# Latent attention: transposed blocks in two PSUM banks, narrow scores in one shared bank

## The chip, the cores and the metric

The program runs on one core of one Trainium2 chip. The metric is the device time of that core in microseconds (us). Three runs of the kernel before took 3803.45, 3799.05 and 3801.53 us; the median is 3801.53 us.

## The reference, cut to what matters

The program is two transformer blocks in one launch. The first has differential attention, a mixture of experts and a pooling mixer. The second runs its layer twice, and each layer has retention, latent attention and gated linear attention side by side. The change lies in the routine that computes both kinds of attention, and moves work in the latent one, which runs twice (once for each layer):

```python
def block(args):                       # one block of 128 queries
    qn, qp, i0 = args
    sc = (jnp.einsum('bqhd,bkhd->bhqk', qn, k_nope)
          + jnp.einsum('bqhd,bkd->bhqk', qp, k_pe)).astype(jnp.float32) * scale
    q_chunk = (i0 + jnp.arange(Q_BLOCK)) // CHUNK
    mask = key_chunk[None, :] <= q_chunk[:, None]
    sc = jnp.where(mask, sc, -jnp.inf)
    p = jax.nn.softmax(sc, axis=-1).astype(v.dtype)
    return jnp.einsum('bhqk,bkhe->bqhe', p, v)
```

There are 8 heads, 1024 positions, 96 columns (64 and 32) in queries and keys, and 64 in values. A block of queries sees the keys of its own chunk of 64 and of those before it.

## The kernel before, in words

`phase_attention` (L610) serves both kinds: `maps == 2` (the flag `diff`) is the differential one, `maps == 1` the latent one, whose tiles are named `mla_...` in the profile. What follows is the latent case.

**Tiling.** A head has 8 tiles of 128 queries. They are taken in pairs, a wide one (tile 7 - i, which sees 8 - i blocks of 128 keys) and a narrow one (tile i, which sees i + 1 blocks), for i = 0 to 3. A step n is one such pair; a head has 4 steps, a phase has 32, and i = n % 4. Every step therefore handles 9 blocks.

**What a step does.** TensorE computes the scores of the pair (`scores`, L734) and adds the mask by a last small product (L751). VectorE takes the negated row maxima, wide first and then narrow (`maxima`, L895, instructions L901 and L909). ScalarE computes the exponentials and their row sums (`exp`, L830, instruction L833). TensorE transposes the blocks of probabilities (L722), ScalarE copies them from PSUM to `aT` (`copy_t`, L826, instruction L828), and TensorE multiplies them by the values (`outputs`, L765, instruction L769). VectorE divides by the row sums (`scaled_out`, L927, instruction L935), which empties `o_ps`. In each step TensorE also transposes half of the keys or of the queries of a later head, the turn (`turn`, L725): at i = 0 the second half of the next head's keys, at i = 1 and 2 its queries, at i = 3 the first half of the keys of the head after it. ScalarE copies turned keys (L823), VectorE turned queries (L884). The last heads have no turn: a phase has 7 turns each at i = 0, 1 and 2, and 6 at i = 3.

**PSUM.** Of the eight banks the scores take six, three for each parity of n: two wide and one narrow. One bank, `tp`, takes all transposed blocks. One, `o_ps`, takes the outputs.

**Order.** Each engine's order is written out by hand. TensorE's (L784 to L811), with its waits:

1. the scores of step n + 1, wide and then narrow (each part waits for the exponentials of the same part two steps earlier; the first step of a head also waits for the copies of its keys and queries, L736);
2. the first four wide blocks of step n are transposed;
3. the narrow outputs of step n - 1, behind a wait for the narrow copy (L774);
4. wait for the copy of the first four; the remaining 4 - i wide blocks are transposed into the same bank;
5. wait for `o_done` (L801), that is for `scaled_out(n - 1)`; then the wide outputs of the first four blocks;
6. wait for the copy of the remaining wide blocks; the turn, into the same bank;
7. the wide outputs of the remaining blocks;
8. wait for the copy of the turn (L810); the i + 1 narrow blocks are transposed.

ScalarE's order in step n is: copy of the first four, exponentials of wide n + 1, copy of the remaining wide blocks, copy of turned keys, copy of the narrow blocks, exponentials of narrow n + 1. VectorE's is: reciprocals (L925), maxima of n + 1 (wide, narrow), `scaled_out(n - 1)`, copy of turned queries. The waits are for counted semaphores. Products of 32-bit tiles show as two records each in the trace, transposes as one.

Of the kernel before, what the change touches and what calls it, by code (L numbers as in the profile page):

```python
# [15 lines left out]
P = 128  # L16
# [6 lines left out]
HEADS = 8  # L23
# [586 lines left out]
def phase_attention(nc, K, name, q, k, v, out, maps, dk, dv, mask, scale, totals, early, lam_parts=None, prefetch=None, out_rows=None):  # L610
# [12 lines left out]
    B0, B1, SM = 0, 4, 8  # L623

# [10 lines left out]
    with Phase(nc, name) as ph:  # L635
# [8 lines left out]
        s_ps = ph.ps("s", [P, 6 * HALF])  # L644
        tp = ph.ps("tp", [P, 4, P])
# [13 lines left out]
        def scores_of(n, part, mp):  # L659

            at = (mp * 2 + (4 - mp) * part if diff else n % 2 * 3 + 2 * part) * HALF
            return s_ps[:, at:at + (tiles_of(n)[part] + 1) * P]
# [9 lines left out]
        with nc.Block() as block:  # L672
# [46 lines left out]
            def _(pe):  # L719
                def transposes(pieces, ready):  # L720
                    for n, piece in enumerate(pieces):
                        last = nc.tensor.transpose(tp[0:piece.shape[-1], n, :], piece, K["ident"])  # L722
                    last.then_inc(ready, 1)

                def turn(what, part, h):  # L725

                    if what == "k":
                        pe.wait_ge(k_in, 16 * h + 16)
                        transposes([ks[:, 4 * part + t, :] for t in range(4)], k_ready)
                    else:  # L730
                        pe.wait_ge(q_in, 16 * h + 16)
                        transposes([qs[:, 4 * part + t, :] for t in range(4)], q_ready)

                def scores(n):  # L734
                    h = n // PAIRS
                    if n % PAIRS == 0:  # L736
# [40 lines left out]
                spare = tp[:, :, :].rearrange("p a b -> p (a b)")  # L777
# [4 lines left out]
                scores(0)  # L782
# [33 lines left out]
            def _(act):  # L816
# [4 lines left out]
                def copy_k(part, h):  # L821
                    act.wait_ge(k_ready, 2 * h + part + 1)
                    act.copy(kT[h % 2][:, part * HALF:(part + 1) * HALF].rearrange("p (n c) -> p n c", n=4),  # L823
                             tp[0:dq, :, :]).then_inc(k_copied, 1)

                def copy_t(n, g, at, count):  # L826
                    act.wait_ge(t_ready, 3 * n + g + 1)
                    act.copy(aT[:, at:at + count, :], tp[:, 0:count, :]).then_inc(t_copied, 1)  # L828
# [20 lines left out]
                copy_k(0, 1)  # L849
# [3 lines left out]
                for n in range(N):  # L853
                    i = n % PAIRS
                    ahead = n + 1 < N
                    copy_t(n, 0, B0, 4)
# [4 lines left out]
                    copy_t(n, 1, B1, 4 - i)  # L861
# [3 lines left out]
                    if what == "k" and h < HEADS:  # L865
                        copy_k(part, h)
                    copy_t(n, 2, SM, i + 1)
# [10 lines left out]
            def _(dve):  # L878
                ch = Chain(dve, own)

                def copy_q(part, h):
# [3 lines left out]
                                      tp[0:dq, :, :], scale, None, ALU.mult).then_inc(q_copied, 1)  # L885
# [2627 lines left out]
```

## Time and profile before

| | |
|---|---|
| median of three runs (lowest, highest) | 3801.53 us (3799.05, 3803.45) |
| span of the profiled execution | 3803.4 us |
| own time of the profiled execution | not listed apart from the span |
| TensorE busy, of the span | 3550.1 us, 93% |
| TensorE weight loads, of the span | 2743.8 us, 72% |
| VectorE / ScalarE / GpSimd busy | 61% / 49% / 9% |
| mean granted TensorE clock | 0.976 |
| the latent-attention phases | about 2677 to 2887 us and 3391 to 3602 us |
| the differential phase | about 294 to 536 us |

The span runs from the first to the last instruction of one profiled execution. It is 1.9 us above the median of the runs and inside their spread, so differences worked out in the trace are taken from the median without a correction. "PEld" is TensorE's loading of the stationary operand, which runs ahead of the products; its rows give the moment at which TensorE reaches a group of instructions. A line of the timeline holds a group of like instructions: its start, the time it covers, the engine, the line, the tile, the shapes and the count. The bracket at its end is idle time of the engine ahead of it, and what ended that.

### The profile page before, as it was taken

Reading aid. Unit: us, or ns where it says so; the run is one execution under the profiler, and the core shown is the slowest. Engines: PE = TensorE matmul, PEld = TensorE weight load, DVE = VectorE, ACT = ScalarE, POOL = GpSimd, SP = SyncE. Lnnn points to the kernel's source line nnn. Section 1 sums busy time; section 2 is a strip of 40 time slices with the busy share of each in tenths; the row PEclk is TensorE's granted clock in tenths of the full one; section 3 lists DMA queues with packets and bytes.
Section 4 is the critical chain, followed back from the end, with each engine's and each line's share of the span. In section 5 each row is a group of like instructions: output and inputs, shape, how many; then the busy total and the mean of one; then the engine's idle time right before and its main releaser. Section 6 shows DMA issues by size and latency. Waiting matters only on the chain. (4 is left out here: it accounts for less than half of the span.)

```text
span 3803.4 us, 53075 instructions
## 1 busy us (share of the span) xinstructions
PE 3550.1 (93%) x18079; PEld 2743.8 (72%) x18079; DVE 2327.9 (61%) x3676; ACT 1876.9 (49%) x3147; POOL 334.8 (9%) x379
## 2 busy tenths in 40 slices
PE   8998889899999989999999998999998989999888
PEld 7885658688777735677887775778775767887666
DVE  3227866699888666548988885750235745313375
ACT  3115652388788610116888884321446623224574
POOL 0000002000000020001000002200002200000032
PEclk9999999899999999999999999999999999999999
DMA  6323224499999885428999997442322344232132
GB/s 241 105 69 101 68 84 167 150 398 398 399 398 399 307 319 206 152 105 300 398 399 398 398 399 288 151 175 68 109 48 80 108 139 171 106 107 63 50 114 81
DMA packets 408607, 781.27 MB, mean 205 GB/s; under 512 B 99296, under 2 KB 154232, under 8 KB 406392
## 3 DMA queue, kind: packets, MB, share of 16 engines
q1 hardware_dynamic: 385400, 695.15, 50.6%
q0 software_dynamic: 13824, 50.34, 3.5%
q10 hardware_dynamic: 9216, 33.56, 2.2%
q8 instruction: 104, 1.70, 0.2%
q14 instruction: 63, 0.52, 0.0%
HBM read 643.00 MB, written 135.95 MB: 205 GB/s over the span
## 5 line engine op out<-in xcount | busy, mean ns | idle before, releaser
L247 DVE TENSOR_TENSOR experts_gate_lo<-weights_gate,experts_gate_hi 128x1024 fp32r<-128x1024 f32 x256 | 300.7, 1221 | 75.3 <-ACT experts_gate_hi L243 62.0
L247 DVE TENSOR_TENSOR experts_down_lo<-weights_down,experts_down_hi 128x1024 fp32r<-128x1024 f32 x256 | 302.2, 1222 | 46.2 <-ACT experts_down_hi L243 42.9
L243 ACT CAST experts_gate_hi<-weights_gate 128x1024 fp32r<-128x1024 f32 x256 | 258.2, 1055 | 125.1 <-DMA weights_gate<-in_moe_w_gate_dram 70.4
L247 DVE TENSOR_TENSOR experts_up_lo<-weights_up,experts_up_hi 128x1024 fp32r<-128x1024 f32 x256 | 297.5, 1219 | 3.3 <-ACT experts_up_hi L243 2.6
L312 PE MATMUL project_acc<-project_wh,project_hh 128*128 128x512 f32 (+2 forms) x768 | 286.3, 373 | 0.0
L314 PE MATMUL project_acc<-project_wh,project_hl 128*128 128x512 f32 (+2 forms) x768 | 282.1, 367 | 0.0
L313 PE MATMUL project_acc<-project_wl,project_hh 128*128 128x512 f32 (+2 forms) x768 | 282.0, 367 | 0.0
L243 ACT CAST experts_up_hi<-weights_up 128x1024 fp32r<-128x1024 f32 x256 | 259.1, 1056 | 43.6 <-DMA weights_up<-in_moe_w_up_dram 41.1
L243 ACT CAST experts_down_hi<-weights_down 128x1024 fp32r<-128x1024 f32 x256 | 260.1, 1052 | 33.9 <-DMA weights_down<-in_moe_w_down_dram 33.2
L2582 ACT COPY project_row<-project_acc 128x512 f32<-128x512 f32 (+2 forms) x96 | 51.9, 541 | 364.3 <-PE project_acc L314 364.3
L312 PE MATMUL experts_gp<-experts_gate_hi,experts_xh 128*128 128x512 f32 x512 | 202.8, 396 | 25.2 <-DVE experts_xl L247 25.1
L312 PE MATMUL experts_yp<-experts_down_hi,experts_hTh 128*128 128x512 f32 x512 | 204.6, 400 | 2.8 <-DVE experts_hTl L247 2.8
L312 PE MATMUL experts_up<-experts_up_hi,experts_xh 128*128 128x512 f32 x512 | 204.9, 400 | 0.0
L901 DVE TENSOR_REDUCE mla_bias<-mla_s 128x1 f32<-128x1024 f32 (+1 forms) x64 | 65.6, 1025 | 225.7 <-PE mla_s L751 225.7
L314 PE MATMUL experts_up<-experts_up_hi,experts_xl 128*128 128x512 f32 x512 | 200.2, 391 | 0.0
L313 PE MATMUL experts_up<-experts_up_lo,experts_xh 128*128 128x512 f32 x512 | 199.8, 390 | 0.0
L314 PE MATMUL experts_gp<-experts_gate_hi,experts_xl 128*128 128x512 f32 x512 | 199.8, 390 | 0.0
L313 PE MATMUL experts_yp<-experts_down_lo,experts_hTh 128*128 128x512 f32 x512 | 199.6, 390 | 0.0
L313 PE MATMUL experts_gp<-experts_gate_lo,experts_xh 128*128 128x512 f32 x512 | 199.5, 390 | 0.0
L314 PE MATMUL experts_yp<-experts_down_hi,experts_hTl 128*128 128x512 f32 x512 | 199.4, 389 | 0.0
L828 ACT COPY mla_aT<-mla_tp 128x384 f32<-128x384 f32 (+1 forms) x192 | 92.0, 479 | 189.7 <-PE mla_tp L722 189.5
L312 PEld LDWEIGHTS project_acc<-project_wh,project_hh 128*128 128x128 f32 x768 | 145.2, 189 | 20.4 <-issue 0.5
(520 smaller groups left out, 8254.7 us busy)
## 6 DMA issues: line engine op xcount, KB each, us to landing
weights_gate<-in_moe_w_gate_dram SPq DMA_DIRECT2D x256, 512.0 KB, 13.4
weights_up<-in_moe_w_up_dram SPq DMA_DIRECT2D x256, 512.0 KB
weights_down<-in_moe_w_down_dram SPq DMA_DIRECT2D x256, 512.0 KB, 13.5
scratch_y<-experts_y ACTq DMA_DIRECT2D x64, 512.0 KB
pool_shared<-in_ada_w_dram SPq DMA_DIRECT2D x16, 1536.0 KB
scratch_proj<-project_row SPq DMA_DIRECT2D x64, 256.0 KB, 2.0
head_store<-in_attn_w_qkv_dram SPq DMA_DIRECT2D x48, 256.0 KB, 3.3
scratch_qkv<-qkv_row SPq DMA_DIRECT2D x48, 256.0 KB, 2.0
```

Of the source, the lines that this page charges most:

```text
L243: return act.copy(hi, src)
L247: return dve.tensor_tensor(lo, src, hi.bitcast(F32), ALU.subtract)
L312: nc.tensor.matmul(acc, a[0][k], b[0][k], start=(start and k == 0), stop=False)
L313: nc.tensor.matmul(acc, a[0][k], b[1][k], start=False, stop=False)
L314: last = nc.tensor.matmul(acc, a[1][k], b[0][k], start=False, stop=(stop and k == n - 1))
L828: act.copy(aT[:, at:at + count, :], tp[:, 0:count, :]).then_inc(t_copied, 1)
L901: dve.tensor_reduce(bias[:, n % 2, mp:mp + 1], scores_of(n, 0, mp), AX.X, ALU.max, negate=True).then_inc(bias_ready, 1)
L2582: act.copy(row[:, n % SLOTS, 0:width(s)], acc[:, n % AB, 0:width(s)]).then_inc(acc_done, 1)
```

## The change

For `maps == 1` alone, `tp` becomes two banks, FRONT and BACK. The first four wide blocks and the turn go to FRONT, the remaining wide blocks and the narrow blocks to BACK. Each group of transposes waits for the copy of the group that used its bank last (`bank_free`). The bank comes from the scores: wide scores keep two banks for each parity, narrow scores of all steps share one, so narrow scores of n + 1 wait for the exponentials of narrow n, and not of n - 1. They are issued behind the transposes of the first four wide blocks of n. The wait for the copy of the first four moves from the remaining transposes to the wide outputs, the wait for the copy of the remaining blocks from ahead of the turn to behind it. For `maps == 2` the number of banks, the order and the conditions stay, and two waits in a step are repeated. The body of TensorE's loop and the helpers (the calls of ScalarE and VectorE change only by the bank they name):

```diff
+    BANKS = 1 if diff else 2
+    FRONT, BACK = BANKS - 1, 0
-        s_ps = ph.ps("s", [P, 6 * HALF])
-        tp = ph.ps("tp", [P, 4, P])
+        s_ps = ph.ps("s", [P, (6 if diff else 5) * HALF])
+        tp = ph.ps("tp", [P, BANKS, 4, P])
...
-            at = (mp * 2 + (4 - mp) * part if diff else n % 2 * 3 + 2 * part) * HALF
+            if diff:
+                at = (mp * 2 + (4 - mp) * part) * HALF
+            else:
+                at = (4 if part else n % 2 * 2) * HALF
...
+                def copied(n, use):
+
+                    if n < 0:
+                        return (k_copied, 3) if use == 3 else None
+                    what, part, ahead = turned(n)
+                    if use != 2:
+                        return t_copied, 3 * n + min(use, 2) + 1
+                    if ahead < HEADS:
+                        return k_copied if what == "k" else q_copied, 2 * ahead + part + 1
+                    return copied(n, use - BANKS)
+
+                def bank_free(n, use):
+                    what = copied(n, use - BANKS) if use >= BANKS else copied(n - 1, use + 4 - BANKS)
+                    if what is not None:
+                        pe.wait_ge(*what)
...
-                def scores(n):
+                def scores(n, parts):
...
-                    before = n - 1 if diff else n - 2
-                    for part, i in enumerate(tiles_of(n)):
+                    for part in parts:
+                        i = tiles_of(n)[part]
+                        before = n - 1 if diff or part else n - 2
...
                     if n + 1 < N:
-                        scores(n + 1)
+                        scores(n + 1, (0, 1) if diff else (0,))
                     a_wait(n, 0)
-                    if n > 0:
-                        pe.wait_ge(t_copied, 3 * n)
-                    else:
-                        pe.wait_ge(k_copied, 3)
-                    transposes(blocks(n, 0, range(4)), t_ready)
+                    bank_free(n, 0)
+                    transposes(FRONT, blocks(n, 0, range(4)), t_ready)
+                    if n + 1 < N and not diff:
+                        scores(n + 1, (1,))
                     if n > 0:
                         narrow_outputs(n - 1)
-                    pe.wait_ge(t_copied, 3 * n + 1)
-                    transposes(blocks(n, 0, range(4, TILES - i)), t_ready)
+                    bank_free(n, 1)
+                    transposes(BACK, blocks(n, 0, range(4, TILES - i)), t_ready)
                     if i == 0:
                         pe.wait_ge(v_in[h % 2], 16 * (h // 2) + 16)
                     if n > 0:
                         pe.wait_ge(o_done, n)
+                    pe.wait_ge(t_copied, 3 * n + 1)
                     outputs(n, 0, range(4), B0)
-                    pe.wait_ge(t_copied, 3 * n + 2)
                     what, part, ahead = turned(n)
                     if ahead < HEADS:
+                        bank_free(n, 2)
                         turn(what, part, ahead)
+                    pe.wait_ge(t_copied, 3 * n + 2)
                     outputs(n, 0, range(4, TILES - i), B0)
                     a_wait(n, 1)
-                    if ahead < HEADS:
-                        pe.wait_ge(k_copied if what == "k" else q_copied, 2 * ahead + part + 1)
-                    transposes(blocks(n, 1, range(i + 1)), t_ready)
+                    bank_free(n, 3)
+                    transposes(BACK, blocks(n, 1, range(i + 1)), t_ready)
```

## Rows read from the trace of the kernel before

**Rows 1.** The page: the span.

```profile
span 3803.4 us, 53075 instructions
```

**Rows 2.** Busy time by stretch: the two latent phases; TensorE, loads, VectorE, ScalarE, GpSimd, clock, DMA.

```profile
2676.80:2887.00 210.20, 191.27 (x1235) 151.70 (x1236) 67.61 (x142) 101.09 (x244) 0.00 (x0) 0.98 0.26 70
3391.00:3602.00 211.00, 190.41 (x1241) 150.39 (x1240) 67.53 (x142) 100.47 (x244) 0.00 (x0) 1.00 0.26 70
```

**Rows 3.** Groups by line, first latent phase: loads for wide, then narrow transposes; idle last.

```profile
L722 PEld LDWEIGHTS mla_tp<-constants,mla_wide 128*128 128x128 f32 x208 | 22.3, 142 | 15.1 <-ACT mla_aT L828 11.0 <-issue 2.8
...
L722 PEld LDWEIGHTS mla_tp<-constants,mla_narrow 128*128 128x128 f32 x80 | 8.8, 144 | 11.0 <-issue 10.8
```

**Rows 4.** Timeline of TensorE's loads, the step n with i = 2 (n + 1 has i = 3).

```profile
2749.63 0.43 PEld L722 LDWEIGHTS mla_tp<-constants,mla_wide 128*128 128x128 f32 x4 [0.24 <-issue]
2750.02 0.53 PEld L769 LDWEIGHTS mla_o_ps<-mla_v,mla_aT 128*128 128x128 f32 x4
2750.97 0.20 PEld L722 LDWEIGHTS mla_tp<-constants,mla_wide 128*128 128x128 f32 x2 [0.42 <-ACT mla_aT L828]
2751.14 0.97 PEld L769 LDWEIGHTS mla_o_ps<-mla_v,mla_aT 128*128 128x128 f32 x8
...
2752.41 0.53 PEld L769 LDWEIGHTS mla_o_ps<-mla_v,mla_aT 128*128 128x128 f32 x4
2753.53 0.31 PEld L722 LDWEIGHTS mla_tp<-constants,mla_narrow 128*128 128x128 f32 x3 [0.59 <-issue]
2753.80 0.30 PEld L748 LDWEIGHTS mla_s<-mla_kT,mla_qT 96*128 96x128 f32 x2
```

**Rows 5.** The same timeline, from the three steps that follow (i = 3, 0, 1).

```profile
2757.72 0.97 PEld L769 LDWEIGHTS mla_o_ps<-mla_v,mla_aT 128*128 128x128 f32 x8 [0.26 <-DVE mla_o L935]
...
2758.99 0.30 PEld L769 LDWEIGHTS mla_o_ps<-mla_v,mla_aT 128*128 128x128 f32 x2
2759.99 0.42 PEld L722 LDWEIGHTS mla_tp<-constants,mla_narrow 128*128 128x128 f32 x4 [0.70 <-issue]
...
2764.56 0.97 PEld L769 LDWEIGHTS mla_o_ps<-mla_v,mla_aT 128*128 128x128 f32 x8 [0.26 <-issue]
...
2770.68 0.97 PEld L769 LDWEIGHTS mla_o_ps<-mla_v,mla_aT 128*128 128x128 f32 x8
2771.66 0.39 PEld L722 LDWEIGHTS mla_tp<-constants,mla_q 128*96 128x96 f32 x4
2772.03 0.75 PEld L769 LDWEIGHTS mla_o_ps<-mla_v,mla_aT 128*128 128x128 f32 x6
2773.14 0.20 PEld L722 LDWEIGHTS mla_tp<-constants,mla_narrow 128*128 128x128 f32 x2 [0.36 <-issue]
```

**Rows 6.** Timeline of VectorE, the same four steps.

```profile
2749.89 0.69 DVE L909 TENSOR_REDUCE mla_bias<-mla_s 128x1 f32<-128x512 f32 x1 [0.15 <-PE mla_s L751]
2750.79 0.29 DVE L935 TENSOR_TENSOR mla_o<-mla_o_ps,mla_ratio 128x128 f32<-128x128 f32 x1 [0.21 <-PE mla_o_ps L769]
2752.72 0.69 DVE L884 TENSOR_SCALAR mla_qT<-mla_tp 96x512 f32<-96x512 f32 x1 [1.64 <-PE mla_tp L722]
...
2757.37 0.29 DVE L935 TENSOR_TENSOR mla_o<-mla_o_ps,mla_ratio 128x128 f32<-128x128 f32 x1
...
2764.16 0.29 DVE L935 TENSOR_TENSOR mla_o<-mla_o_ps,mla_ratio 128x128 f32<-128x128 f32 x1 [0.48 <-PE mla_o_ps L769]
...
2769.44 0.55 DVE L909 TENSOR_REDUCE mla_bias<-mla_s 128x1 f32<-128x384 f32 x1
2770.03 0.29 DVE L935 TENSOR_TENSOR mla_o<-mla_o_ps,mla_ratio 128x128 f32<-128x128 f32 x1
```

**Rows 7.** Timeline of ScalarE: end of the longest narrow exponentials, and the copy after the first scores.

```profile
2755.07 0.20 ACT L833 ACTIVATION_READ_ACCUMULATOR mla_narrow<-mla_s,mla_bias 128x1 f32 x1
...
2685.80 0.59 ACT L828 COPY mla_aT<-mla_tp 128x512 f32<-128x512 f32 x1 [3.29 <-PE mla_tp L722]
```

**Rows 8.** Timeline of TensorE's loads: the first wide outputs of the phase.

```profile
2686.83 0.97 PEld L769 LDWEIGHTS mla_o_ps<-mla_v,mla_aT 128*128 128x128 f32 x8
```

More of the change, by code:

```diff
@@ L719, in _, with transposes @@
             def _(pe):
-                def transposes(pieces, ready):
+                def transposes(bank, pieces, ready):
                     for n, piece in enumerate(pieces):
-                        last = nc.tensor.transpose(tp[0:piece.shape[-1], n, :], piece, K["ident"])
+                        last = nc.tensor.transpose(tp[0:piece.shape[-1], bank, n, :], piece, K["ident"])
                     last.then_inc(ready, 1)
+                def copied(n, use):
[11 more added lines that the diff above has]
+                        pe.wait_ge(*what)
                 def turn(what, part, h):
@@ L728, in turn @@
                         pe.wait_ge(k_in, 16 * h + 16)
-                        transposes([ks[:, 4 * part + t, :] for t in range(4)], k_ready)
+                        transposes(FRONT if h > 1 or part else BACK, [ks[:, 4 * part + t, :] for t in range(4)], k_ready)
                     else:
                         pe.wait_ge(q_in, 16 * h + 16)
-                        transposes([qs[:, 4 * part + t, :] for t in range(4)], q_ready)
-                def scores(n):
+                        transposes(FRONT, [qs[:, 4 * part + t, :] for t in range(4)], q_ready)
+                def scores(n, parts):
                     h = n // PAIRS
-                    if n % PAIRS == 0:
+                    if n % PAIRS == 0 and 0 in parts:
                         pe.wait_ge(k_copied, 2 * h + 2)
                         pe.wait_ge(q_copied, 2 * h + 2)
-                    before = n - 1 if diff else n - 2
-                    for part, i in enumerate(tiles_of(n)):
+                    for part in parts:
+                        i = tiles_of(n)[part]
+                        before = n - 1 if diff or part else n - 2
                         if before >= 0:
@@ L775, in narrow_outputs @@
                     outputs(n, 1, range(n % PAIRS + 1), SM).then_inc(o_ready, 1)
-                spare = tp[:, :, :].rearrange("p a b -> p (a b)")
+                spare = tp[:, FRONT, :, :].rearrange("p a b -> p (a b)")
                 pe.sem_inc(k_ready, 2)
@@ L781, in _ @@
                     pe.wait_ge(masks_ready, 2)
-                scores(0)
+                scores(0, (0, 1))
                 turn("k", 0, 1)
@@ L819, in _, with copy_k, copy_t @@
                     act.copy(maskr[:, :], mask).then_inc(masks_ready, 1)
-                def copy_k(part, h):
+                def copy_k(bank, part, h):
                     act.wait_ge(k_ready, 2 * h + part + 1)
                     act.copy(kT[h % 2][:, part * HALF:(part + 1) * HALF].rearrange("p (n c) -> p n c", n=4),
-                             tp[0:dq, :, :]).then_inc(k_copied, 1)
-                def copy_t(n, g, at, count):
+                             tp[0:dq, bank, :, :]).then_inc(k_copied, 1)
+                def copy_t(n, g, bank, at, count):
                     act.wait_ge(t_ready, 3 * n + g + 1)
-                    act.copy(aT[:, at:at + count, :], tp[:, 0:count, :]).then_inc(t_copied, 1)
+                    act.copy(aT[:, at:at + count, :], tp[:, bank, 0:count, :]).then_inc(t_copied, 1)
                 def exp(n, part, mp):
@@ L848, in _ @@
                         exp(0, part, mp)
-                copy_k(0, 1)
+                copy_k(BACK, 0, 1)
                 if diff:
@@ L855, in _ @@
                     ahead = n + 1 < N
-                    copy_t(n, 0, B0, 4)
+                    copy_t(n, 0, FRONT, B0, 4)
                     if diff and n > 0:
@@ L860, in _ @@
                         exp(n + 1, 0, 0)
-                    copy_t(n, 1, B1, 4 - i)
+                    copy_t(n, 1, BACK, B1, 4 - i)
                     if ahead and diff:
@@ L865, in _ @@
                     if what == "k" and h < HEADS:
-                        copy_k(part, h)
-                    copy_t(n, 2, SM, i + 1)
+                        copy_k(FRONT, part, h)
+                    copy_t(n, 2, BACK, SM, i + 1)
                     if ahead:
@@ L884, in copy_q @@
                     dve.tensor_scalar(qT[h % 2][:, part * HALF:(part + 1) * HALF].rearrange("p (n c) -> p n c", n=4),
-                                      tp[0:dq, :, :], scale, None, ALU.mult).then_inc(q_copied, 1)
+                                      tp[0:dq, FRONT, :, :], scale, None, ALU.mult).then_inc(q_copied, 1)
                 def masked(n, part):
```

## The prediction, made before the changed kernel was run

> **What bounds the kernel now.** I read the page first for the span, 3803.4 us [rows 1], then the busy time in the two stretches of latent attention. There TensorE's products are busy 191.27 us of 210.20 and 190.41 of 211.00; VectorE has 67.61 and ScalarE 101.09 in the first [rows 2]. So TensorE sets the pace, and its two neighbours matter only where it waits for them. The two phases are alike, so one is worked out and doubled. What can be won is TensorE's waits, and the groups by line tell where these are: of the idle time of the loads in one phase, 15.1 us lie ahead of the transposes of wide blocks (11.0 of them ended by ScalarE's copy) and 11.0 ahead of the transposes of narrow blocks [rows 3]. These are two waits for the one transposing bank, one early and one late in each step. The timeline shows both: a bracket of 0.42 at the remaining wide transposes and of 0.59 at the narrow ones, in the step with i = 2 [rows 4].
>
> The product's busy time says that 19 us of a phase are open. The Trainium skill ("Perfetto Trace Analysis", Identifying the Most-Contended Engine) calls this a bad measure and wants the busy share of the loads, here 151.70 of 210.20 [rows 2], which would leave 58 us open. The brackets at the transposes, 26.1 us together [rows 3], stand nearer to the first. I use neither share and follow single steps.
>
> **Part 1: narrow transposes no longer wait for the copy of the turn.** They get a bank of their own, and the wait there goes. What each costs now is read between groups of loads; a pair of output loads advances TensorE by 0.22 us (eight take 0.97, of which the last is 0.19, so 0.11 each).
> - i = 3: loads at 2758.99, two of them, so the transposes could start at 2759.21; they start at 2759.99 [rows 5]. 0.78 us gone.
> - i = 1: 2772.03 plus six loads is 2772.69; they start at 2773.14 [rows 5]. 0.45 us gone.
> - i = 2: 2752.41 plus four is 2752.85, against 2753.53 [rows 4]. But this turn is the last half of the next head's queries, and the next thing on TensorE is that head's scores, which need it. VectorE's copy ends at 2752.72 + 0.69 = 2753.41 [rows 6]. The three transposes fit into the gap; the scores follow at about 2753.55 in place of 2753.80. 0.25 us gone, and the rest of the wait stays, now at the scores.
> - i = 0: the idle time of rows 3 is used up by the others (7 x 0.36 + 7 x 0.59 + 6 x 0.70 = 10.85 of 11.0), so nothing.
> A phase has 7, 7 and 6 of these: 7 x 0.45 + 7 x 0.25 + 6 x 0.78 = 9.6 us gained.
>
> **Part 2: remaining wide transposes no longer wait for the copy of the first four.** This wait goes as well, but the outputs behind it also wait for `o_done`, that is for VectorE to empty the previous outputs, and VectorE does this behind both maxima of n + 1. So the question is when `scaled_out` (L935) ends. Up to the narrow outputs of n - 1, TensorE has the same work in the other order, so those end when they do now. But the narrow scores are finished later, by the four transposes now ahead of them: 0.39 us (2749.63 to 2750.02, rows 4). That moves the narrow maximum, and with it `scaled_out`. For the four steps, by i of n + 1:
> - i = 3: the narrow maximum now starts at 2749.89, when its scores come (the bracket names them), and would start at 2750.28. It takes 0.69 and, by the pair at 2769.44 (0.55 long, followed 0.59 later), L935 follows 0.73 later, at 2751.01, and ends at 2751.30. Now L935 ends at 2751.08 and the outputs start at 2751.14 [rows 4, 6]. Lost: about 0.22.
> - i = 0: the narrow maximum waits for the wide one anyway; L935 ends at 2757.66 and the outputs start at 2757.72 as now [rows 5, 6]. Nothing.
> - i = 1: L935 waits for the narrow outputs (bracket 0.48) and not for a maximum; its end, 2764.45, and the outputs' start, 2764.56, stay [rows 5, 6]. Nothing.
> - i = 2: the maximum at 2769.44 moves to about 2769.72 (its scores come some 0.1 ahead of it now), L935 ends at 2770.60 in place of 2770.32, and the outputs start at 2770.66, as against 2770.68 [rows 5, 6]. Nothing, though the wait of 0.6 us that stood ahead of them is gone.
> So the early wait is not saved: it turns from one for ScalarE's copy into one for VectorE. This is the step of the argument on which most hangs. The turn behind it, with i = 1, starts at 2771.66 where eight loads from 2770.68 would end at 2771.56 [rows 5]; that wait moves behind the turn, where the copy has long been done: 0.10 gained, 8 times.
>
> **Part 3: one more wait at a place where TensorE has stopped.** The outputs wait for `o_done` and then for the first copy. Loads follow the event by 0.06 us where it ends a single wait (2757.66 to 2757.72) and by 0.11 or 0.12 where two waits stand together (2764.45 to 2764.56; 2753.41 to 2753.53) [rows 4 to 6]. I take 0.05 for it in each step, between nothing (the second wait is met and read behind running work) and 0.12. With part 2: per head 0.22 + 4 x 0.05 = 0.42, eight times, 3.4 us lost.
>
> **Part 4: the shared narrow bank.** Narrow scores of n + 1 now wait for narrow exponentials of n. The longest end at 2755.07 + 0.20 = 2755.27 [rows 7], while TensorE is in 1024 columns of wide scores that it began at 2753.80 and that keep it until about 2755.6; the four transposes come on top. Part 1 moves both by about the same. Cost nothing, with some 0.7 us to spare; if that were used up, it would stop TensorE once a step. The queues of DMA are not passed by anything that moves.
>
> **Part 5: start and the other attention.** In the first step no `o_done` is awaited. The outputs start at 2686.83 where the copy of the first four ended at 2685.80 + 0.59 [rows 7, 8]: 0.4 us gained at least, up to about 1.3 as the copy itself comes earlier; I take 0.4. The differential phase gets two repeated waits in a step, both for things awaited just before; nothing, between a gain of nothing and a loss of 32 x 0.1 = 3.2 us.
>
> **Sum.** 9.6 + 0.8 - 3.4 + 0.4 = 7.4 us a phase, 14.8 us in both. The span of 3803.4 would be 3788.6; the profiled execution lies 1.9 us above the median of 3801.53, inside the runs' spread, so I take the same from the median: 3786.7, rounded to 3786.
>
> **Rivals.**
> *The early wait is saved too.* If `scaled_out` is not what holds the outputs, for instance because VectorE gets at it sooner than I chain it, the 11.0 us of rows 3 come on top of part 1, and part 3 costs nothing: 9.6 + 11.0 + 0.4 = 21.0 a phase, 3759. Against it: at i = 2 `scaled_out` ends only 0.3 us ahead of the outputs today, and at i = 0 and 1 it is what they wait for. Chance 0.08.
> *Slower: the narrow maximum delays `scaled_out` in every step.* If the wide maximum covers none of the 0.39 us, each of 32 steps loses 0.39 + 0.05, 14.1 us a phase against 9.6 + 0.4: 4.1 lost, 8.2 in both, 3810. It decides from a mean shift above 0.31 us a step. For it speaks i = 3; against it, in two of four steps the row ahead of L935 has room. Chance 0.08.
> *Waits cost on the path.* The change adds two waits to each of 64 latent and 32 differential steps, 192. At 0.05 each, all on the path, this is 9.6 us, of which 3.2 are in the sum: 3786 + 6 = 3792; at 0.12 it is 23 us, and the change makes no difference, 3802 to 3806. Against it: the transposes at 2749.63 go over to the narrow outputs at 2750.02 through a met wait in no more than four loads take [rows 4]. The Trainium skill ("Advanced Engine Details and Errata", Network/Comms) gives 50 to 100 ns for reading a semaphore from a sequencer, which speaks for this case; 192 at the upper figure would be an estimated 19 us; only the stops of part 3 bear it out. Chance of a time within 0.2% of before by this or by a wait that takes part 1's place: 0.12.
>
> **How the numbers follow.** The forecast has 0.72. A measurement of this kernel tells about 0.2%, 7.6 us, from no change, so faster means under 3794. Faster: 0.72 and 0.08. The range takes in the unknown prices around the sum: part 3 at nothing, the start at 1.3 and no loss at i = 3 give 3786 - 3.2 - 1.8 - 3.5 = 3777, and half of the first rival's early wait would bring it to 3770; part 3 at 0.12 and the differential waits give 3786 + 4.5 + 3.2 = 3794, and the third rival reaches 3800. I give 3769 to 3800.
>
> **What the profile would show.** The idle time ahead of narrow transposes falls from 11.0 us a phase to near nothing, and some 0.4 us appears ahead of the scores of each head. The idle time ahead of remaining wide transposes that ScalarE ended goes too, and about as much appears ahead of the wide outputs, ended by VectorE's L935. Each phase is 7 to 8 us shorter; the differential phase is as long as before. I am wrong if the wide outputs start without a wait, if TensorE stops at the narrow scores, or if L935 ends later in steps other than i = 3.

## The result, and the profile after

The changed kernel takes 3773.49 us (median of four runs, 3767.24 to 3777.52), against 3800.29 us for the kernel before in the same comparison. The ratio is 0.9927, 95% interval 0.9915 to 0.9938: 26.8 us faster, where 14.8 were forecast. The time lies inside the stated range, the direction is right, and the size is short by almost half.

The profiled span fell by more, from 3803.4 to 3765.4 us. So the first reading is where the 38.0 us lie. I measured each latent phase from the first load of the scores (L748 before, L770 after) to the first load of the warm-up products behind the last outputs (L322).

| us | before | after | less |
|---|---|---|---|
| up to the first latent phase | 2676.87 | 2672.29 | 4.6 |
| first latent phase | 208.96 | 194.05 | 14.9 |
| between | 509.15 | 508.59 | 0.6 |
| second latent phase | 206.04 | 192.33 | 13.7 |
| behind it | 202.38 | 198.14 | 4.2 |

The phases hold 28.6 us, about what the medians show; the rest lies outside the changed code, and the experiments tell whether it belongs to the change. In the first phase the profile of before also has TensorE at a granted clock of 0.66 for its first 5.2 us and 0.87 for the next 13: within them lie 6.8 us at the lower of its two levels (0.50, that is 1.2 GHz), from 2678.5 on. TensorE had waited 2.84 us ahead of the phase's first load, in both profiles. The profile after has 1.00 in both stretches, but TensorE waits 2.08 us there for the first load of keys, against 0.32 before. So the second phase, at 1.00 in both profiles, is the clean comparison: 13.7 us, where 7.4 were forecast.

Busy time in the two phases after the change; the columns are those of rows 2:

```profile
2672.29:2866.34 194.05, 182.29 (x1232) 144.99 (x1232) 66.45 (x141) 103.46 (x240) 0.00 (x0) 1.00 0.28 76
3374.93:3567.26 192.33, 182.29 (x1232) 144.99 (x1233) 66.46 (x141) 102.09 (x239) 0.00 (x0) 1.00 0.28 76
```

The differential phase did not move: from its first load of the scores to its last of the outputs it takes 249.3 us before and 249.4 after. Over 294 to 536 us, TensorE is busy 208.53 us before and 208.43 after.

Then the waits. Groups by line in the first latent phase, loads alone, idle time last; they answer to [rows 3]:

```profile
L791 PEld LDWEIGHTS mla_o_ps<-mla_v,mla_aT 128*128 128x128 f32 x573 | 71.0, 191 | 19.9 <-DVE mla_o L957 12.8 <-ACT mla_aT L850 3.5 <-issue 2.2
L727 PEld LDWEIGHTS mla_tp<-constants,mla_wide 128*128 128x128 f32 x208 | 24.0, 150 | 3.0 <-issue 1.7
...
L727 PEld LDWEIGHTS mla_tp<-constants,mla_narrow 128*128 128x128 f32 x80 | 10.4, 164 | 0.0
```

Ahead of the narrow transposes 11.0 us have become 0.0. Ahead of the wide ones 15.1 have become 3.0. But ahead of the outputs, where the same view of before had 5.2 us (2.1 of them ended by L935), there are now 19.9, and 12.8 of these are ended by L957, which is VectorE's division (L935 before) under its new line number. The late wait is gone, and the early one stands elsewhere, as the prediction said.

One step on VectorE and TensorE, n with i = 2, which answers to [rows 4] and to the first two of [rows 6]:

```profile
2761.49 0.42 PEld L727 LDWEIGHTS mla_tp<-constants,mla_wide 128*128 128x128 f32 x4
...
2763.11 0.69 DVE L931 TENSOR_REDUCE mla_bias<-mla_s 128x1 f32<-128x512 f32 x1 [0.56 <-PE mla_s L773]
2763.24 0.26 PEld L727 LDWEIGHTS mla_tp<-constants,mla_wide 128*128 128x128 f32 x2
...
2763.72 0.28 DVE L957 TENSOR_TENSOR mla_o<-mla_o_ps,mla_ratio 128x128 f32<-128x128 f32 x1
...
2764.05 0.97 PEld L791 LDWEIGHTS mla_o_ps<-mla_v,mla_aT 128*128 128x128 f32 x8 [0.55 <-DVE mla_o L957]
...
2765.71 0.37 PEld L727 LDWEIGHTS mla_tp<-constants,mla_narrow 128*128 128x128 f32 x3
...
2766.39 0.30 PEld L770 LDWEIGHTS mla_s<-keep 96*128 96x128 f32 x2 [0.30 <-issue]
```

TensorE reaches the remaining wide transposes at 2763.24 without a bracket and then stops for the division until 2764.05, 0.05 us behind the division's end. The narrow transposes at 2765.71 stand without a bracket, and what is left of the wait for the queries is 0.30 ahead of the scores.

The length of a step, from the first load of wide scores to the next such load, gives the gain by step. It is named by i of step n, whose turn and narrow transposes end it: i = 3, 6.58 to 5.77 us; i = 0, 6.49 to 6.36; i = 1, 6.44 to 5.74; i = 2, 6.34 to 6.12. A head went from 25.85 to 23.99 us, 1.86 less.

### The profile page after: what moved, and what is told of

Same layout as the page of the kernel before. It is cut to its first block and busy times, and to the rows that moved or that the text cites. A ratio compares the mean times of both kernels' runs of the same rounds, so it can differ in the third digit from the quotient of the medians.

```text
span 3765.4 us, 53163 instructions
## 1 busy us (share of the span) xinstructions
PE 3538.7 (94%) x18079; PEld 2734.9 (73%) x18079; DVE 2327.0 (62%) x3676; ACT 1883.9 (50%) x3147; POOL 332.7 (9%) x379
## 3 DMA queue, kind: packets, MB, share of 16 engines
q8 instruction: 105, 1.72, 0.2%
## 5 line engine op out<-in xcount | busy, mean ns | idle before, releaser
L791 PE MATMUL mla_o_ps<-mla_v,mla_aT 128*128 128x64 f32 x1152 | 158.2, 275 | 17.9 <-DVE mla_o L957 14.4
L791 PEld LDWEIGHTS mla_o_ps<-mla_v,mla_aT 128*128 128x128 f32 x1152 | 142.7, 191 | 39.4 <-DVE mla_o L957 25.7
```

What stands on the lines that cost most here:

```text
L791: mm = nc.tensor.matmul(o_ps[:, 1 - part, 0:dv], aT[:, at + j, :], vs[:, n // PAIRS % 2, j, :], start=(j == 0), stop=(j == last_j))
```

## The experiments

All are compared with the kernel before on the same chip. Phases are given as first and second, measured as above; the changed kernel has 194.05 and 192.33 in its first profile.

**The changed kernel again.** No edit.

> The changed kernel once more, as the yardstick for the others on this chip. Measured in its trace so far, from the first load of the scores to the first load of the warm-up products behind the last outputs: 194.07 us in the first latent phase and 192.33 in the second, against 208.96 and 206.04 before, so 28.6 us less in both. The profiled spans differed by 38.0 us and the medians by 26.8. Theory: the phases alone are the gain, and what stands apart from them between two profiles is scatter between executions. Expected: both phases within 0.3 us of 194.07 and 192.33, time 0.990 to 0.995 of before. Rival: other phases are shorter too, because the latent ones end earlier; then the last phase, 202.4 before and 198.1 after from the end of the second latent one to the end of the span, is again 4 us shorter.

Measured: 0.9926 (0.9909 to 0.9942), median 3772.64 us; phases 194.32 and 192.39. The stretch behind the second phase took 198.20 us. In the nine other profiles of this study it took 198.3 to 202.5 us: 202.36 in the run with four more waits, whose phases are those of the changed kernel, 198.34 in the last one. So this stretch scatters by 4 us between executions, whatever the order in the phases, and the phases are the gain. Differences under 4 us are read from the phases alone, below.

**The narrow bank alone.** The remaining wide blocks go to FRONT, behind the old wait, and the narrow scores go back ahead of the transposes (ScalarE's copy, and the wait in a step without a turn, name the bank to match; not shown):

```diff
-                        scores(n + 1, (0, 1) if diff else (0,))
+                        scores(n + 1, (0, 1))
...
-                    if n + 1 < N and not diff:
-                        scores(n + 1, (1,))
...
-                    bank_free(n, 1)
-                    transposes(BACK, blocks(n, 0, range(4, TILES - i)), t_ready)
+                    pe.wait_ge(t_copied, 3 * n + 1)
+                    transposes(FRONT, blocks(n, 0, range(4, TILES - i)), t_ready)
...
-                        bank_free(n, 2)
+                        pe.wait_ge(t_copied, 3 * n + 2)
```

> Part 1 alone: the narrow blocks have a bank of their own, and all wide blocks and the turn share the other one, with the waits of before. Narrow scores stay ahead of the transposes, in one shared bank. My theory (the late wait is most of the gain, steps as corrected by the trace of the changed kernel: 0.12, 0.45, 0.25 and 0.78 us for i = 0 to 3): 10.4 us less than before in each phase, phases of 198.6 and 195.6, time about 3779, and the idle time of the wide loads ended by ScalarE stays at about 11 us a phase. Rival (the two waits share the gain evenly, or the early one has most): 7 us or less in each phase.

Measured: 0.9943 (0.9926 to 0.9959), median 3780.13 us; phases 196.94 and 195.26, so 12.0 and 10.8 us less than before. Waits of TensorE's loads in its first phase (what waited, for whom, us in total, times, longest):

```profile
PEld mla_tp L727 <- ACT mla_aT L848: 11.2, 25, 0.9
```

The early wait is whole, 11.2 us where the kernel before has 11.0, and the time is still 0.6% shorter. Part 1 was sized nearly right: 10.8 in the clean phase against 9.6 predicted and 10.4 by the corrected steps. The rival of an even share is out.

**The early wait alone.** The changed kernel, with the wait for the copy of the turn put back ahead of the narrow transposes:

```diff
                     bank_free(n, 3)
+                    if ahead < HEADS:
+                        pe.wait_ge(k_copied if what == "k" else q_copied, 2 * ahead + part + 1)
```

> Part 2 alone: two alternating banks and the narrow scores behind the transposes, but the narrow transposes wait for the copy of the turn as before. My theory in the prediction was that this part gains nothing and loses 1.3 us a phase to the later narrow maximum and 1.6 to a second wait. The trace of the changed kernel puts it at a gain of about 4 us a phase. Expected by the corrected theory: phases of 204 to 205.5 and 201 to 202.5. By the predicted one: 209 to 212. By the rival that the early wait of 11.0 us is saved whole: 198 and 195.

Measured: 0.9985 (0.9975 to 0.9994), median 3794.25 us; phases 204.97 and 203.40, so 4.0 and 2.6 us less than before. The prediction's loss of 2.6 us a phase is refuted, and so is the saving of the whole 11 us. With 10.8 from the run above the clean phase adds up to 13.4 of 13.7: two parts, nearly independent. Part 2's gain includes the start of the phase (part 5), since no step of that is undone here.

**Four more waits in a step.** All are for events already awaited, so they only cost their own handling:

```diff
+                    pe.wait_ge(t_copied, 3 * n + 1)
+                    pe.wait_ge(t_copied, 3 * n + 1)
                     outputs(n, 0, range(4), B0)
...
                     bank_free(n, 3)
+                    pe.wait_ge(t_copied, 3 * n + 2)
+                    pe.wait_ge(t_copied, 3 * n + 2)
```

> The changed kernel with four further waits in every step of all three attention phases, all for events already awaited: two ahead of the first wide outputs, where TensorE stops for VectorE, and two ahead of the narrow transposes. 384 more waits. By part 3 of the prediction (0.05 us for each wait behind a stop, here two a step) the latent phases are 3.2 us longer each and the time 6 to 10 us. By the rival that each wait costs on the path: 0.05 to 0.12 for each of 384, 19 to 46 us. By the trace of the changed kernel, where the outputs start 0.05 us behind the end of the VectorE instruction though two waits stand there: nothing, phases within 0.3 us of 194.07 and 192.33.

Measured: 0.9923 (0.9906 to 0.9939), median 3771.00 us; phases 192.70 and 192.57. The second is 0.2 us longer than the changed kernel's, over 32 steps with 128 more waits; the first is 1.4 us shorter, since TensorE waited only 0.7 us for the first load of keys there, and 2.1 in the changed kernel's first profile. Two rows of its timeline, the division and the loads behind it:

```profile
2736.97 0.28 DVE L961 TENSOR_TENSOR mla_o<-mla_o_ps,mla_ratio 128x128 f32<-128x128 f32 x1
...
2737.31 0.97 PEld L791 LDWEIGHTS mla_o_ps<-mla_v,mla_aT 128*128 128x128 f32 x8 [0.55 <-DVE mla_o L961]
```

The division ends at 2737.25 and the loads start at 2737.31, 0.06 later, though the program has four waits there. The trace tells why: the added waits do not stand behind the stop. They show as semaphore instructions of TensorE, 0.05 us each, and those of the two added lines ahead of the outputs come more than 1 us before the loads of these outputs in this step (i = 2), and as a rule 0.6 to 0.9 us before them at i = 1 and 3:

```profile
L824 PEldq EVENT_SEMAPHORE  x1: 51/51/51, 2736.1 to 2736.1; - x1
L825 PEldq EVENT_SEMAPHORE  x1: 51/51/51, 2736.2 to 2736.2; - x1
```

The page counts 192 more instructions than for the changed kernel, for 384 more waits. So the waits are there, and they are handled while TensorE still has work: that costs nothing which can be measured. At i = 0, where a wait for the values stands there too, one of them shares the instruction that stops for the division; the loads follow the division's end by 0.07 us there, as in the changed kernel. What a further instruction behind the stop would cost, this run does not test. Part 3 of the prediction and the third rival fall together, because the change puts no further instruction behind a stop. So does the weight given there to the figure of the Trainium skill ("Advanced Engine Details and Errata", Network/Comms), 50 to 100 ns for reading a semaphore: 128 times 50 ns would be an estimated 6.4 us a phase, and the clean phase shows 0.2.

**All wide blocks in one bank, order kept.** As the narrow bank alone, but with the narrow scores left where the change puts them, so that order and banks come apart (the wait ahead of the turn and ScalarE's copy follow, as there):

```diff
-                    bank_free(n, 1)
-                    transposes(BACK, blocks(n, 0, range(4, TILES - i)), t_ready)
+                    pe.wait_ge(t_copied, 3 * n + 1)
+                    transposes(FRONT, blocks(n, 0, range(4, TILES - i)), t_ready)
```

> The changed kernel, order and narrow bank kept, but the remaining wide blocks go into the same bank as the first four, behind a wait for their copy; so the two banks no longer alternate. Theory: what removes the early wait is the order, since narrow scores and narrow outputs now lie between the two groups of transposes and give ScalarE the time: the copy of the first four ends about 1.3 us behind the start of their transposes, and TensorE comes to the remaining ones 1.3 to 1.8 us behind it. Expected: phases of 194 to 195 and 192.3 to 193.3 (changed: 194.3 and 192.4), time as the changed kernel. Rival: the alternating banks are what removes it; then some of the 11 us a phase come back and the phases are about those of narrow_bank_alone, 196.9 and 195.3.

Measured: 0.9928 (0.9911 to 0.9946), median 3774.15 us; phases 194.46 and 192.79. Within 0.5 us of the changed kernel. With this order one bank is enough to keep ScalarE's copy of the first four off TensorE's path: the narrow scores and the narrow outputs lie between the two groups. The alternation of the wide groups gives 0.5 us a phase on top, and 0.4 of that lie in the first step (5.95 us against 5.57), in which no division is awaited. Against the narrow bank alone, from which only the order differs, the phases are 2.5 us shorter.

**The narrow scores first again.** The changed kernel with both banks, but the old place of the narrow scores (the first two pieces of the diff of the narrow bank alone).

> The changed kernel with the narrow scores back ahead of the transposes of the first four blocks; both transposing banks and the shared narrow bank stay. This undoes what delays the narrow maximum. Theory: the division then waits for the narrow outputs in every step, which end when they do in the changed kernel; at i = 2 and 3 of n + 1 it starts 0.15 and 0.10 us earlier, so each phase is 2 us shorter, 192.3 and 190.3, and no early wait comes back, since the outputs wait for the division anyway. At i = 3 the shared bank may cost 0.1 us, as the narrow exponentials end just when the narrow scores could start. Rival by the prediction's price for that step (0.22 a head plus the waits): 3.4 us a phase shorter. Rival that the order is what saves the early wait: 4 us or more a phase longer.

Measured: 0.9936 (0.9920 to 0.9953), median 3777.25 us; phases 194.66 and 192.69. A miss: 2 us a phase shorter was expected, and it is 0.3 to 0.6 longer, by either profile of the changed kernel. The division does start earlier, by the 0.15 and 0.10 us expected:

```profile
2742.74 0.20 ACT L853 ACTIVATION_READ_ACCUMULATOR mla_narrow<-mla_s,mla_bias 128x1 f32 x1
...
2742.99 0.30 PEld L770 LDWEIGHTS mla_s<-keep 96*128 96x128 f32 x2
...
2762.13 0.42 PEld L727 LDWEIGHTS mla_tp<-constants,mla_wide 128*128 128x128 f32 x4
...
2762.83 0.59 ACT L848 COPY mla_aT<-mla_tp 128x512 f32<-128x512 f32 x1 [1.82 <-PE mla_tp L727]
...
2763.10 0.29 DVE L955 TENSOR_TENSOR mla_o<-mla_o_ps,mla_ratio 128x128 f32<-128x128 f32 x1
...
2763.53 0.97 PEld L791 LDWEIGHTS mla_o_ps<-mla_v,mla_aT 128*128 128x128 f32 x8 [0.47 <-DVE mla_o L955]
2763.56 1.08 PE L791 MATMUL mla_o_ps<-mla_v,mla_aT 128*128 128x64 f32 x8 [0.26 <-ACT mla_aT L848]
```

At 2763.10 it starts 1.73 us behind the wide scores (that is, behind the first load that follows theirs), where the changed kernel has 1.88. But the outputs start 0.14 us behind its end at 2763.39 and not 0.05. ScalarE's copy of the first four, whose transposes now come later, ends at 2763.42, and the products of the outputs name it as what they waited for. So the copy is next in line and takes back more than half of the gain at this step. At i = 3 of n + 1 the narrow scores start at 2742.99, 0.05 us behind the end of the narrow exponentials at 2742.94: the shared bank costs the 0.1 us that was flagged. So both orders are nearly even, and whichever of the two comes first delays the other's consumer.

Four of the runs now make a square, and it tells what removes the early wait. Second phase, us:

| | wide blocks in one bank | in two |
|---|---|---|
| narrow scores ahead of the transposes | 195.26 | 192.69 |
| behind them | 192.79 | 192.33 |

The order alone takes 2.5 off, the second bank for the wide blocks alone 2.6, and both 2.9. So either is nearly enough, and the changed kernel has both.

**Moving VectorE's division.** If the wide outputs wait for the division, the division can be moved. Three kernels, on top of the changed one. First, VectorE divides between the two maxima:

```diff
                                           negate=True).then_inc(bias_ready, 1)
+                    if between is not None:
+                        scaled_out(between)
                     dve.wait_ge(s_ready, 2 * n + 2)
...
+                    early = not diff and n > 0 and n + 1 < N
...
-                        maxima(n + 1)
+                        maxima(n + 1, n - 1 if early else None)
...
-                    if not diff and n > 0:
+                    if not diff and n > 0 and not early:
                         scaled_out(n - 1)
```

> The changed kernel with VectorE dividing the outputs of n - 1 between the wide and the narrow maximum of n + 1, in place of behind both. Theory: in the changed kernel the wide outputs wait for this division, and it starts behind the narrow maximum at i = 2 and 3 of n + 1, 0.15 to 0.25 us later than the narrow outputs would allow. Expected: 2 to 3.5 us less in each phase, 191 to 192 and 189 to 190.5. Rival: the division is bound by the narrow outputs alone; then no difference.

Measured: 0.9923 (0.9906 to 0.9939), median 3769.89 us; phases 191.98 and 190.43. 2 us a phase less than the changed kernel, at the edge of what was expected. In its profile the division waits for TensorE's narrow outputs in every step. At i = 2 and i = 3 of n + 1 it starts 1.73 and 2.13 us behind the wide scores, where the changed kernel has 1.88 and 2.23, and the gain lies there:

```profile
2736.99 0.29 DVE L959 TENSOR_TENSOR mla_o<-mla_o_ps,mla_ratio 128x128 f32<-128x128 f32 x1 [0.51 <-PE mla_o_ps L791]
...
2742.80 0.29 DVE L959 TENSOR_TENSOR mla_o<-mla_o_ps,mla_ratio 128x128 f32<-128x128 f32 x1 [1.07 <-PE mla_o_ps L791]
```

At i = 0 and 1 the narrow outputs bound the division already: there it stays at 1.72 and 2.16 us.

Second, the narrow outputs go ahead of the narrow scores and VectorE keeps its order:

```diff
+                    if n > 0:
+                        narrow_outputs(n - 1)
                     if n + 1 < N and not diff:
                         scores(n + 1, (1,))
-                    if n > 0:
-                        narrow_outputs(n - 1)
```

> The changed kernel with the narrow outputs of n - 1 ahead of the narrow scores of n + 1. The division could start earlier, but VectorE's order puts it behind the narrow maximum, whose scores come later by the narrow outputs (0.22 to 0.88 us). Theory: the division starts later by 0.25, 0.26, 0.22 and 0.44 us at i = 0 to 3, so each phase is about 9 us longer, 203 and 201. Rival (the narrow outputs alone bound the division): 5 to 10 us less in each phase.

Measured: 0.9979 (0.9969 to 0.9988), median 3792.06 us; phases 202.19 and 200.67, so 8.1 and 8.3 us longer than the changed kernel, where 9 were expected. This is the slower rival of the prediction, provoked: at i = 0 to 3 of n + 1 the division starts 0.14, 0.28, 0.22 and 0.44 us later than in the changed kernel, and the wide outputs later by the same to 0.01.

Third, both:

> Both of the last two: narrow outputs ahead of narrow scores, and the division between the maxima. Theory: now the division starts behind the wide maximum or 0.33 us behind the narrow outputs, whichever is later: 1.40, 1.60, 1.14 and 1.16 us behind the wide scores at i = 0 to 3, against 1.72, 2.15, 1.88 and 2.23 in the changed kernel; the wide outputs then start 0.33, 0.27, 0.52 and 0.51 us earlier. 1.6 us a head, 13 us a phase: 181 and 179.5, time about 26 us under the changed kernel, 3747. Rival: another wait takes its place at once (copy of the first four, or of the remaining wide blocks behind the exponentials); then less than 6 us a phase.

Measured: 0.9862 (0.9845 to 0.9878), median 3746.94 us, against an expected 3747; phases 180.71 and 179.54 against 181 and 179.5. The mechanism holds too: the division starts 1.41, 1.61, 1.14 and 1.16 us behind the wide scores at i = 0 to 3 of n + 1, where 1.40, 1.60, 1.14 and 1.16 were expected. One edit alone gives 2 us a phase, the other costs 8, and both together give 13. Waits of the loads from 2700 to 2850 us in this kernel:

```profile
PEld mla_s L770 <- issue: 14.8, 60, 0.3
PEld mla_s L773 <- issue: 3.1, 13, 0.2
PEld mla_tp L727 <- issue: 3.1, 13, 0.2
PEld mla_o_ps L791 <- DVE mla_o L959: 1.1, 6, 0.2
PEld mla_o_ps L791 <- ACT mla_aT L850: 0.2, 1, 0.2
```

The waiting for the division is down to 1.1 us in this stretch, and over the whole first phase from 12.8 us in the changed kernel to 1.8. What is left is "issue": mostly the 0.24 us between the loads of 512-column products that are still running, and 0.3 a head ahead of the scores that need new queries. TensorE is busy 176.84 of 179.54 us in the second phase.

**The same with one wide bank.** The last kernel with all wide blocks and the turn in one bank.

> The fastest version so far (narrow outputs ahead of narrow scores, division between the maxima; phases of 180.7 and 180.1) with all wide blocks and the turn in one transposing bank, the narrow blocks in the other. Theory: as in wide_in_one_bank, the work between the two groups of transposes covers the copy of the first four; phases within 0.8 us of 180.7 and 180.1. Rival: with the wait for the division gone, the early wait shows; 3 us or more a phase longer.

Measured: 0.9873 (0.9857 to 0.9890), median 3751.96 us; phases 183.95 and 182.51, so 3.2 and 3.0 us longer (the expectation has 180.1 for the second phase of the kernel it starts from; its trace has 179.54). That is the rival's size, but not the rival's wait. Waits of the loads over the same stretch:

```profile
PEld mla_tp L727 <- ACT mla_aT L850: 1.4, 6, 0.2
PEld mla_o_ps L791 <- DVE mla_o L959: 1.2, 7, 0.2
```

A wait for ScalarE's copy is back, but it is not the early one, for the copy of the first four. The six stand ahead of the turn, which shares its bank with the remaining wide blocks here and waits for their copy:

```profile
2748.55 0.97 PEld L791 LDWEIGHTS mla_o_ps<-mla_v,mla_aT 128*128 128x128 f32 x8 [0.18 <-DVE mla_o L959]
2749.74 0.39 PEld L727 LDWEIGHTS mla_tp<-constants,mla_k 128*96 128x96 f32 x4 [0.23 <-ACT mla_aT L850]
```

In the kernel with two banks this turn starts 0.83 us behind the first load of the outputs, here 1.19. In every step but the first the wide outputs start as early as there (1.74, 2.22, 1.66 and 1.98 us behind the wide scores), so the theory was right on the copy of the first four and overlooked the turn. In the first step, where no division is awaited, the early wait does show: 5.95 us against 5.57. In the changed kernel the later outputs gave the copy of the remaining blocks the time. So the alternation of the wide groups is worth 0.5 us a phase in the changed kernel and about 3 in this one.

## Why the prediction was right, and where it was off

The direction, the mechanism and the place of both waits were right; the size was a little over half. By its own steps, for the clean phase, where 6.3 us of 13.7 were missing:

- **Part 1, the late wait (9.6 us a phase).** Alone it gave 10.8 in the clean phase. Most of the rest is the turn at i = 0, which I set to nothing because the idle time of a group by line was used up by the others; its step was 0.13 us shorter, 7 times. So a wait can show no idle time ahead of a load and still delay the next group. i = 3 gave 0.78 in this run, as predicted (0.81 in the changed kernel).
- **Part 2, the early wait turns into one for VectorE.** Right, and this was the step on which most hung: 12.8 us of the loads' idle time are now ended by the division. Mis-sized was its price at i = 3 of n + 1: 0.22 us lost, by "L935 follows 0.73 later". I took that from the pair at 2769.44 and 2770.03 in [rows 6], as if the division had waited for the maximum. In the changed kernel a maximum of 0.56 us is followed by the division after 0.47, and one of 0.69 after 0.61. So at 2770.03 it had been waiting for the narrow outputs, without a bracket since VectorE was never idle. The run with the division between the maxima bears this out: there it starts at the same 1.73 us behind the wide scores as in the kernel before, and the bracket names the narrow outputs. The outputs start 2.56 us behind the wide scores where they had 2.48: 0.08 lost, not 0.22. At i = 2 the outputs start at 2.22 where they had 2.38: 0.16 gained, where I had 0.02. The last sign of being wrong, L935 later in a step other than i = 3, did show at i = 2 (1.88 for 1.73), but part 2 itself had it move there, and by more.
- **Part 3, a second wait behind a stop (0.05 us a step, 1.6 a phase).** Nothing, by the run with four more. The price was read from real rows, but it does not carry over. In the kernel before, the wait for the division is an instruction of its own only at i = 0, where a wait for the values stands beside it: L801 appears 21 times, seven in each of the three attention phases. It starts 0.04 us behind the division's end and takes 0.05, and the load follows 0.02 later:

```profile
L801 PEldq EVENT_SEMAPHORE  x1: 51/51/51, 2764.5 to 2764.5; - x1
```

In the changed kernel it is the added wait, for the copy of the first four (L823), that is an instruction of its own, and it is handled 1.2 us ahead of the outputs of the step shown above (2764.05):

```profile
L823 PEldq EVENT_SEMAPHORE  x1: 51/51/51, 2762.8 to 2762.8; - x1
```

At i = 0 that instruction holds the wait for the division as well, starts 1.1 us before the division's end, and the loads follow this end by 0.07 us where they had 0.12. Why L801 starts only behind it stays open. In the other steps the loads follow by 0.05.

- **Part 4, the shared narrow bank.** Nothing, as predicted: the changed kernel shows no wait of the narrow scores. The bank has no slack once the narrow scores come first: there they wait and lose 0.1 us at i = 3 of n + 1.
- **Part 5.** The differential phase is unchanged (249.3 and 249.4 us in the two profiles; 245.3 to 250.6 over all twelve). The first step, from the wide scores of step 1 to those of step 2, fell from 6.38 to 5.57 us in the clean phase: 0.8 gained, where I took 0.4 between 0.4 and 1.3.

The parts 2 and 3 together were predicted as a loss of 2.6 us a phase. The run of the early wait alone gave a gain of 2.6 in the clean phase, of which 0.8 are the start, so about 1.8 are theirs: 4.4 of the 6.3 that were missing. The 1.2 of part 1 and 0.4 of the start are nearly the rest. At the low end of the range, half of the first rival's early wait is 5.5 us a phase, so it brings 3777 to 3766 and not to 3770; the measured time lies above both. The first rival (3759, the 11 us of the early wait saved too) is refuted: in the changed kernel TensorE waits for the division instead. The slower one acts at i = 3, as was said, and the run that provokes it in every step lost 8 us a phase. That a range of 31 us held the time says little for the sum; the waits named in it, and where they went, are what came out right.

The measure of what is open was too small as well. TensorE's products were idle for 19.1 us of the clean phase before (busy 186.91 of 206.04), and the best version takes 26.5 us off: their busy time itself fell, to 176.84.

## What to carry to other kernels

A buffer that removes a wait pays only up to the next event that ends at nearly the same time, so for each wait that goes, work out when its neighbours end and who is queued ahead of them on their engines. Here a second bank for the wide blocks was worth 2.6 us a phase with the narrow scores in their old place, half a microsecond once the order alone gave ScalarE the time, and three once the division was out of the way, then at another wait, that of the turn. What a buffer is worth belongs to the order around it. Change both orders at once where one feeds the other: the two halves of the best version gave 2 us less and 8 us more alone, and 13 us less together.

## What the runs showed of the hardware that was not expected

- A wait already met is free on TensorE where it is handled behind running work: 128 more in a phase changed it by 0.2 us, and the trace has those ahead of the wide outputs, at i = 1 to 3, mostly 0.6 to 1.2 us before these start. The loads follow the end of the division by 0.05 us where no instruction of its own waits for it, and by 0.07 or 0.12 where one does.
- VectorE starts its next instruction before the recorded end of a row reduction: 0.09 us before with 384 columns, 0.08 with 512. A row's duration is then not the distance to the next start, and an instruction without idle time ahead of it may still have waited for another engine during the overlap.
- The stretch behind the second latent phase, unchanged in every kernel, took 198.1 to 202.5 us in twelve profiles, and the granted clock at the start of the first latent phase was 0.66 in one profile and 1.00 in the other eleven. A difference of two spans alone, 38.0 us here, would have overstated the change by a third.
